# TensorE operands at multiples of 512 bytes, and the last attention pair's units and splits in another order

## The reference

```python
# even layer: one input product, two branches, one output product
z = u_lat @ w_in                                     # 1024 x 8192
y_a = z[AB] * dwconv(z[AC] * z[AX], w_conv, 1) * silu(z[AG])
s = concat([q @ k_win + bias, q @ k_ctx]); p = softmax(s)
y_b = (p_win @ v_win + p_ctx @ v_ctx) * silu(z[BG])
h = h + gate * (concat([y_a, y_b]) @ w_out)          # 2048 x 1024, latents and context

# odd layer: 8 blocks of 256 channels
x = dwconv(z[:, :2048], conv_w, 1) + conv_b
r, i = sigmoid(x @ w_ra + b_ra), sigmoid(x @ w_ri + b_ri)      # for each direction and block
a = exp(8 * r * log_sigmoid(lam)); b = sqrt(1 - a**2) * i * x
y = scan_forward(a, b) + scan_backward(a, b)
h = h + gate * ((y * silu(z[:, 2048:])) @ w_out)
out = rmsnorm(h) * final_g
```

## Time and profile before

| | |
|---|---|
| device time, median of 3 runs | 2328.14 us (2328.09 to 2329.01) |
| the profiled execution | 2327.99 us, span 2326.2 us, TensorE clock granted 0.991 |
| TensorE matmuls busy | 2254.2 us, 97% |
| VectorE, ScalarE, GpSimd busy | 1505.7 (65%), 1168.1 (50%), 493.5 us (21%) |
| even layer, pairs | 80 to 1262 us |
| output projection, two passes | to 1498 us |
| odd layer, block loop | 1552 to about 2135 us |
| final product | to 2326 us |

### The profile page before, as it was taken

One profiled execution on the slowest core, in us unless ns is written; L12 is line 12 of the kernel. 1 busy time (PEld: TensorE's weight loads), 2 busy tenths in 40 slices (PEclk: granted clock), 3 DMA queues, 4 the chain that ended last, 5 costly groups with the idle time before them and its releaser, 6 DMA issues. The chain is left out here.

```text
span 2326.2 us, 33502 instructions
## 1 busy us (share of the span) xinstructions
PE 2254.2 (97%) x11996; PEld 1910.1 (82%) x11996; DVE 1505.7 (65%) x2407; ACT 1168.1 (50%) x1696; POOL 493.5 (21%) x287
## 2 busy tenths in 40 slices
PE   6999999999999999999998999799999999999998
PEld 4788888888888888888886788688888888887787
DVE  4576575765757657577567536648667766776765
ACT  4534444345344453444434244347876787678311
POOL 0232231322323323233221030022222222220000
PEclk9999999999999999999998999899999999999999
DMA  7111221111112111122223756201111111113521
GB/s 292 37 54 52 66 61 66 54 52 62 54 59 72 52 57 59 34 70 70 66 63 121 214 168 180 85 31 55 56 54 55 55 46 64 55 55 127 208 82 64
DMA packets 146665, 187.50 MB, mean 81 GB/s; under 512 B 50520, under 2 KB 109144, under 8 KB 143448
## 3 DMA queue, kind: packets, MB, share of 16 engines
q1 hardware_dynamic: 138888, 166.67, 22.7%
q10 hardware_dynamic: 7632, 18.88, 2.2%
HBM read 155.62 MB, written 29.88 MB: 80 GB/s over the span
## 5 line engine op out<-in xcount | busy, mean ns | idle before, releaser
L1390 PE MATMUL ps<-u_hi,w_hi 128*128 128x512 f32 (+1 forms) x1464 | 533.2, 364 | 0.0
L1390 PE MATMUL ps<-u_hi,w_lo 128*128 128x512 f32 (+1 forms) x1464 | 519.9, 355 | 0.0
L1390 PE MATMUL ps<-u_lo,w_hi 128*128 128x512 f32 (+1 forms) x1464 | 517.8, 354 | 0.0
L1390 PEld LDWEIGHTS ps<-u_hi,w_lo 128*128 128x128 f32 x1464 | 276.4, 189 | 40.1
L1390 PEld LDWEIGHTS ps<-u_lo,w_hi 128*128 128x128 f32 x1464 | 277.1, 189 | 35.2
L1390 PEld LDWEIGHTS ps<-u_hi,w_hi 128*128 128x128 f32 x1464 | 276.5, 189 | 35.2
L2322 PE MATMUL ps<-u_hi,o_w_hi 128*128 128x512 f32 (+1 forms) x640 | 240.0, 375 | 9.4 <-POOL o_w_lo L1897 9.4
L732 ACT ACTIVATE probs<-probs,neg_max 128x640 f32<-128x640 f32 (+1 forms) x160 | 122.7, 767 | 248.5 <-DVE neg_max L1062 248.5
L1897 POOL TENSOR_TENSOR o_w_lo<-o_w_raw,o_w_hi 128x1024 fp32r<-128x1024 f32 x48 | 143.0, 2979 | 466.7 <-ACT o_w_hi L1916 466.7
L2322 PE MATMUL ps<-u_hi,o_w_lo 128*128 128x512 f32 (+1 forms) x640 | 238.7, 373 | 0.0
L2322 PE MATMUL ps<-u_lo,o_w_hi 128*128 128x512 f32 (+1 forms) x640 | 238.3, 372 | 0.0
(11 more groups left out here) (247 smaller groups left out, 4612.8 us busy)
## 6 DMA issues: line engine op xcount, KB each, us to landing
w_stage<-in_w_even SPq DMA_DIRECT2D x63, 512.0 KB, 3.8
o_w_raw<-in_w_odd SPq DMA_DIRECT2D x48, 512.0 KB, 3.7
ada_piece<-in_w_ada SPq DMA_DIRECT2D x20, 1024.0 KB, 5.9
y_raw<-y_scratch SPq DMA_DIRECT2D x40, 512.0 KB, 6.2
wout_raw<-in_w_out SPq DMA_DIRECT2D x16, 512.0 KB, 5.9
y_scratch<-h_backward SPq DMA_DIRECT2D x16, 512.0 KB, 3.0
final_w_raw<-in_w_out SPq DMA_DIRECT2D x8, 1024.0 KB, 11.4
final_y_raw<-y_scratch SPq DMA_DIRECT2D x15, 512.0 KB, 4.6
```

Of the source, the lines that this page charges most:

```text
L1390: last = nc.tensor.matmul(ps[:, bank(j, g), 0:t - f], w[:, slot, c * P:(c + 1) * P], x[:, c, f:t], start=(c == 0 and n == 0), stop=(c == K ...
```

## The change

1. `Map.align` rounds to 512 bytes from the base (`LINE`), and rows that TensorE reads get lengths to fit (`XCOLS` 1312 to 1408). All of TensorE's operands but probs and probs_t (at 256) then start at byte 128 of a 512-byte line: the stacks, x_tiles, wout1, x_hi, x_lo and o_w_lo. Small tiles move into the gaps of x_hi and x_lo, others elsewhere.
2. In the last pair, unit 8 goes from step 5 to step 6, unit 10 is done in two halves (steps 7 and 8), tile 0's chunks are cut 6, 5, 5 in place of 5, 6, 5, and the splits of w_out go to other places.
3. The gate diagonals are made by ScalarE (four ACTIVATE each) in place of VectorE.
4. In the odd layer, ScalarE's split of GW0 goes from the end of a block's list to between the first and the second evacuation of the next one's.

```diff
-        self.at = (self.at + P - 1) // P * P
+        self.at = (self.at + LINE - 1) // LINE * LINE
-ODD_RAW = Map.TOP - Map.BASE - 3 * KC * P * 4
+ODD_RAW = (Map.TOP - Map.BASE) // LINE * LINE - 3 * KC * P * 4
-LAST_UNITS = ((0,), (1,), (2, 3), (4,), (5, 6), (7, 8), (9,), (10,), (11,))
+LAST_UNITS = (((0, 0, 8),), ((1, 0, 8),), ((2, 0, 8), (3, 0, 8)), ((4, 0, 8),), ((5, 0, 8), (6, 0, 8)), ((7, 0, 8),),
+              ((8, 0, 8), (9, 0, 8)), ((10, 0, 4),), ((10, 4, 8), (11, 0, 8)))
-OUT_CHUNKS = {9: (0, 0, 5), 10: (0, 5, 11), 11: (0, 11, YC), ...
+OUT_CHUNKS = {9: (0, 0, 6), 10: (0, 6, 11), 11: (0, 11, YC), ...
-XCOLS = 1312
+XCOLS = 1408
...
@@ ScalarE, even layer
+            def gate_diagonal(pass_, s):
+                for c in range(4):
+                    ins = nc.scalar.activation(diag[:, s, c * P:(c + 1) * P], k["ident"][:], ACT.Copy,
+                                               scale=k["modx"][:, 4 * pass_ + c, s:s + 1])
+                ins.then_inc(diag_done, 1)
...
@@ ScalarE, even layer, behind(s)
                 elif s == 11:
                     out_y_hi(1, 1, 0)
+                    act.wait_ge(ya_stored, 32 * PAIRS + 16)
+                    gate_diagonal(0, 0)
...
@@ VectorE, even layer, within(s)
-                if s == 7:
-                    out_w_lo(0)
-                    out_w_lo(1)
-                elif s == 8:
+                if s == 9:
                     out_w_lo(2)
-                elif s == 9:
-                    out_w_lo(4)
+                    out_w_lo(3)
                 elif s == 10:
                     out_y_lo(0, 0, 1)
-                    out_w_lo(6)
+                    out_w_lo(5)
+                elif s == 11:
+                    out_w_lo(7)
...
@@ VectorE, ahead(s)
-                if s == 8:
+                if s == 7:
+                    out_w_lo(0)
+                elif s == 8:
                     out_y_lo(0, 0, 0)
...
@@ VectorE, behind(s)
-                if s == 8:
-                    out_w_lo(3)
+                if s == 7:
+                    out_w_lo(1)
                 elif s == 9:
-                    out_w_lo(5)
+                    out_w_lo(4)
                 elif s == 10:
-                    out_w_lo(7)
+                    out_w_lo(6)
...
@@ ScalarE, odd layer
             def body(n, last):
-                for g in range(1, NG):
-                    evacuate(n, X1, g)
+                evacuate(n, X1, 1)
+                split_hi(n, GW0)
+                evacuate(n, X1, 2)
...
                     evacuate(n + 1, X1, 0)
                     x_hi(n, 0)
-                    split_hi(n + 1, GW0)
```

More of the change, by code:

```diff
@@ L77, in split_at_ctx @@
     return [(a, b)]
+LINE = 512
 class Map:
@@ L204, in even_layer @@
     pt = m("probs_t", [P, KEYS // P, 2 * P], F32R)
+    low_at = m.at
+    small, th = m("c_cols", [P, KC, 2]), m("c_tanh", [P, KC, 2])
+    ss, rms, rinv = m("sum_squares", [P, NT]), m("rms", [P, NT]), m("rms_inverse", [P, NT])
+    m.at = low_at
     low, t2 = m("pv_low", [P, 2 * P]), m("pv_out", [P, P])
     negmax, sums, rcp = m("neg_max", [P, 2]), m("row_sums", [P, 2]), m("row_rcp", [P, 2])
-    small, th = m("c_cols", [P, KC, 2]), m("c_tanh", [P, KC, 2])
-    ss, rms, rinv = m("sum_squares", [P, NT]), m("rms", [P, NT]), m("rms_inverse", [P, NT])
     assert Map.BASE + m.at <= Map.TOP - 2 * KC * P * 4 - SILU_BYTES
@@ L261, in even_layer @@
     xh = over("x_half", [P, 2, 512], ada_at + 2 * 512 * 4)
[L262 to L266, removed]
+    row_at = ada_at + 4 * 512 * 4
+    ut = over("u_tile", [P, KC, P], row_at)
+    grow = over("gate_rows", [P, 2, 2, 512], row_at + 2 * 512 * 4)
+    diag = over("gate_diag", [P, 2, 512], row_at + 6 * 512 * 4)
+    ones = over("gate_ones", [P, P], row_at + 8 * 512 * 4)
+    assert row_at + 8 * 512 * 4 + P * 4 <= x_at
     y1hi = over("y_hi1", [P, KC, 2 * P], Map.BASE + PHASE, F32R)
@@ L355, in pieces @@
         if last:
-            return [(*ORDER[u], 0, KC) for u in LAST_UNITS[s]] if s < len(LAST_UNITS) else []
+            return [(*ORDER[u], c0, c1) for u, c0, c1 in LAST_UNITS[s]] if s < len(LAST_UNITS) else []
         return [(j, g, 0, KC) for j, g in (ORDER[s:s + 1] if s < STEPS - 1 else ORDER[s:])]
@@ L998, in projection @@
                     store_half(t)
+                    if t == 3:
+                        act.wait_ge(row_mm, 2)
+                        for v in range(2):
+                            gate_diagonal(1, v)
                     if t >= 6:
@@ L1690, in odd_layer @@
     m = Map(nc, PHASE)
-    convw, convb = m("conv_w4", [P, 64]), m("conv_b4", [P, 16])
-    grow, ones = m("final_gate_row", [P, D]), m("final_ones", [P, P])
-    lru, lam = m("lru_columns", [P, 5, 32]), m("lam", [P, 32])
+    grow, lru = m("final_gate_row", [P, D]), m("lru_columns", [P, 5, 32])
     bri, bra, L, Lh, nLh = (lru[:, q, :] for q in range(5))
-    own = m("lru_block_columns", [P, 5, 2, 2])
-    e_, z_, z2, den, low = (m(x, [P, 32]) for x in ("log_e", "log_z", "log_z2", "log_den", "log_low"))
     ss, var = m("final_ss", [P, NLT, 2]), m("final_var", [P, NLT])
@@ L1717, in odd_layer @@
     wlo = m("o_w_lo", [P, 3, KC * P], F32R)
+    gaps = [X_AT + (q * XCOLS + QCOLS + 4) * 4 for q in range(3)]
+    m.at = gaps[0]
+    convw, convb, lam = m("conv_w4", [P, 64]), m("conv_b4", [P, 16]), m("lam", [P, 32])
+    assert m.at <= X_AT + XCOLS * 4
+    m.at = gaps[1]
+    own = m("lru_block_columns", [P, 5, 2, 2])
+    e_, z_, z2 = (m(x, [P, 32]) for x in ("log_e", "log_z", "log_z2"))
+    assert m.at <= X_AT + 2 * XCOLS * 4
+    m.at = gaps[2]
+    den, low = (m(x, [P, 32]) for x in ("log_den", "log_low"))
+    assert m.at <= X_END
     def over(name, shape, at, dt=F32):
@@ L1739, in odd_layer @@
     junk = over("final_squares", [P, 512], D * 4)
-    diag = over("final_diag", [P, KC * P], H0_AT)
+    diag, ones = over("final_diag", [P, KC * P], H0_AT), over("final_ones", [P, P], H1_AT)
     def y_raw(q):
```

54 lines of the change are left out of this document (23 added, 31 removed).

## The result

The changed kernel takes 2333.82 us (median of 11 runs, 2331.94 to 2336.19), the kernel before 2328.80 on the same chips (11 runs, 2327.37 to 2329.48): 1.0026 of it, 95% interval 1.0018 to 1.0035. It is slower by 5 us. The forecast was 2325; the measured time is rival A's, 2333.5, with a chance of 0.30. The order that decided in the odd layer stood in the prediction, but the wrong one of two was taken as the likelier; the last pair cost about 1 us more than its term.

What follows compares the result with a forecast made beforehand. In the odd loop, TensorE's chain and the ScalarE/VectorE chain to x_lo were taken as equally long. 2327.99 - 2.5 - 0.7 - 1.1 - 0.5 + 1.9 = 2325.1, plus 0.15: 2325 us; own range 2318 to 2329, overall 2311 to 2337.

Steps and rivals of the forecast that it cites:

- rival A: Odd layer's block loop: GpSimd's split gets in one operation earlier, x_lo 1.1 us later per block; 2333.5 us, chance 0.30.
- the last pair: Even layer's last pair: probs_t wait shrinks, a new 2.2 us wait for w_lo(7) appears; +1.9 us, between -4 and +5.
- Pass 1: Output projection, pass 1: new addresses save 5.3 ns on each of 480 matmuls, -2.5 us.
- TensorE's own share: Odd layer's block loop: new addresses speed projection pieces by 0.92 and gate pieces by 0.28 us, together -1.2 per block.
- So the loop keeps 0.1 us per block: Odd layer's block loop: only matmuls on the chain to x_lo count; seven blocks give -0.7 us, between 0 and -8.4.
- Prologue and last block: Odd layer's prologue and last block: the same piece gains over about one and a half blocks, -1.1 us.
- Even layer: Even layer, pairs before the last: only the attention stacks move, 256 to 128; -0.5 us taken, up to -4.9.
- Diagonals: Gate diagonals on ScalarE: VectorE loses four operations, 0.87 us, ScalarE gains as many; 0 taken, +0.5 if transposition is delayed.

## Why the prediction was wrong

Item by item, by its own steps.

1. Pass 1, -2.5 us: 118.6 to 116.1, -2.5. Right.
2. TensorE's own share, -1.2 per block: 5.48 for 24 (5.45 forecast), 24.70 for 120 in place of 25.17, 6.90 for 36 gates in place of 6.97. With Z0's split on VectorE the block went to 77.33, -0.86, and 0.25 of the rest is still the wait for x_lo: about -1.1. Right.
3. **The step that failed**: "So the loop keeps 0.1 us per block". It rested on the order of GpSimd's request for Z0 and L2137 staying as it was, though the working under rival A had the request 0.42 us ahead. It came 0.32 ahead, having moved 0.44 against L2137 where 0.12 is enough, and a block became 1.17 us longer (forecast 1.1), 8.2 over seven. The doubt that I set against it, that a request had been seen to win only between the scans, was no reason: the scans, L2142 and L2137 are all operations of one engine with two inputs in SBUF, and the rows show a hold at each (4.31 us for 2.35, 2.27 for 1.50, 3.57 for 1.50). I had the sum right, and gave the case that it pointed to the smaller chance.
4. Prologue and last block, -1.1: -1.2 to the first gate and -0.4 at the end. Right, 0.5 better.
5. Even layer, -0.5: nothing in these two executions (1126.9 both); over all kernels 1126.9 to 1128.2 with the stacks at byte 256 (three) and 1125.7 to 1127.2 at 128 (ten), so 1 us is possible and not shown. The slower first matmuls behind attention do not come from the stacks' addresses: the first five 512-column distances are 231 ns on average in both kernels, against 226.7 from the eleventh on.
6. The last pair, +1.9 between -4 and +5: its own run +3.0 (1.0005 to 1.0023 of 2327, 1.2 to 5.4 us), in the profile +3.8. The waits came where they were named: 2.19 us for the last split (2.2 forecast) and one for w_lo(2). Mis-sized were the wait for w_lo(2) itself, 1.55 us, named without a figure, and the wait for u_lo, which grew from 3.39 to 4.06 where I had it fall; and the wait ahead of tile 0's first chunk grew by 0.8, which the prediction has nowhere.
7. Diagonals: four ACTIVATE take 1.26 us together; by themselves they were not tried, so no run shows the 0 of this item.

Sum by what was measured: 2327.99 - 2.5 + 8.2 - 1.6 + 0 + 3.8 = 2335.9, and the profiled execution took 2336.19. Its 2334.3 us of span stand 8.1 above the kernel before, the medians of 11 runs only 5.0; the stretch of the last pair and pass 0 differs by 3.3 us between two kernels that are the same there (152.7 in the changed kernel, 149.4 in the run with Z0's split later). The granted clock from 1224 to 1266 is 0.84 in the one and 0.88 in the other, 13.6 and 10.2 us at the lower level, and of these two the wait of 1.55 us is in the changed kernel alone.

Rival A's mechanism and its 1.1 us per block are right, but that its total of 2333.5 meets the median within 0.3 us is partly luck: its other terms are 2 us off in sum against the profiled execution (last pair +3.8 for +1.9, prologue and last block -1.6 for -1.1, even layer 0 for -0.5).

The Trainium skill (SBUF — State Buffer, SBUF: two separate sides) says that of such an operation of VectorE and one of GpSimd whoever starts first holds the shared ports for the whole instruction: the traces agree, 1.50 against 3.57 us by whoever comes first. By the Trainium skill's rule for the distance between matmuls (TensorE: Matmul & The Clock Gate, Back-to-back issue gap) the addresses would have bought nothing; the measurement decides otherwise, 227 ns with o_w_lo at bytes 128 and 384 against 232 to 236 beside it at the three others.

## What to carry to other kernels

Where two chains end within 0.2 us of each other, a faster engine is worth next to nothing until the other chain is shortened, and it can turn an order elsewhere: list the requests to a shared resource with their distance from what they may overtake, and take the side to which the sum falls. A hold of GpSimd costs VectorE least where VectorE waits anyway, and a subtraction that VectorE does itself in such a pause may cost less than the hold. A shift of 0.44 us between two requests was worth 8 us here in one direction; taking the split off GpSimd, with the same addresses, 12 in the other (from 3.1 above the kernel before to 9.0 below). And a TensorE that is busy for the whole of a stretch may still be held by another chain: the start of its weight load, right behind what it needs, says so where the busy time doesn't.

## What the runs showed of the hardware

o_w_lo, whose 128 columns of fp32 TensorE loads as weights, gives 227 ns per 128x512 matmul if it starts at byte 128 or 384 of a 512-byte line; at 0, 192 or 480 it slows the matmuls beside it to 232 to 236 (ahead of it at 192 to 229). wout1, which TensorE streams past the loaded operand, shows the same: 232.2 ns at byte 256, 226.9 at 128. I had expected multiples of 512 from the base to be needed, as the change has them; for o_w_lo 256 did.

GpSimd's request is served between two operations of VectorE that stand 0.03 us apart (L2150 ends at 1769.71, L2155 is entered at 1769.74 and lasts 3.57). Which comes first is settled to 0.03 us: 3.73 us for L2155 with the request 0.02 ahead, 1.50 with it 0.01 behind.
